# Attention exponentials behind the weights' copies, steps one product later, a new order in the last group, row factors on ScalarE

## The reference

```
proj = rms_norm(x, g_mix) @ w_in            # q,k,v,z,beta,a | qd,kd,vd | gate_a,gate_b
oa = gated_delta_rule(...)                  # chunked, with a triangular inverse per head
oa = rms_norm(oa, g_delta_out) * silu(za)
p  = softmax(qd @ kd^T / 8 + bias)          # two maps per head, 8 heads, causal
od = (p[0] - lam * p[1]) @ vd
od = rms_norm(od, g_subln) * (1 - lam_init) # per token and head
mix = sigmoid(gate_a + b0) * oa + sigmoid(gate_b + b1) * od
x = x + mix @ w_o
x = x + moe_ffn(rms_norm(x, g_ffn))         # top 4 of 32 experts, width 1024, clamped SwiGLU
```

## Time and profile before

| | |
|---|---|
| median of 3 runs | 1276.15 us (1274.95 to 1277.62) |
| the profiled execution | 1277.58 us, its span 1275.9 us, mean granted clock 0.997 |
| busy: PE, DVE, ACT, POOL | 1220.6, 391.1, 308.3, 43.3 us |
| moved | 465.59 MB, 364 GB/s over the span |
| chain that ended last | PE 65%, DMA 19%, DVE 5%, ACT 3% |
| largest lines of the chain | 2037 20%, loads of w_up 19%, 2084 14%, 1747 6%, 1978 and 1698 4% each |

### The profile page before, as it was taken

One profiled execution on the slowest core, in us unless ns is written; L12 is line 12 of the kernel. 1 busy time (PEld: TensorE's weight loads), 2 busy tenths in 40 slices (PEclk: granted clock), 3 DMA queues, 4 the chain that ended last, 5 costly groups with the idle time before them and its releaser, 6 DMA issues.

```text
span 1275.9 us, 14962 instructions
## 1 busy us (share of the span) xinstructions
PE 1220.6 (96%) x5558; PEld 535.2 (42%) x5558; DVE 391.1 (31%) x1041; ACT 308.3 (24%) x644; POOL 43.3 (3%) x100
## 2 busy tenths in 40 slices
PE   9999999999999999999999999999999999999997
PEld 7777456644443333333333333333333333333332
DVE  5776647479341221111221111221111112211111
ACT  3332222464222121121121112121121211111121
POOL 4401000000000000000000000000000000000000
PEclk9999999999999999999999999999999999999999
DMA  7644974698969999999999999999999999999997
GB/s 257 185 156 131 226 234 150 156 299 303 380 257 423 426 429 428 429 428 428 428 429 427 429 429 429 428 428 427 429 429 428 428 427 429 428 429 428 429 426 303
DMA packets 67582, 465.59 MB, mean 365 GB/s; under 512 B 11016, under 2 KB 14216, under 8 KB 42848
## 3 DMA queue, kind: packets, MB, share of 16 engines
q1 hardware_dynamic: 61768, 452.68, 86.1%
q0 software_dynamic: 5344, 11.95, 4.9%
q10 hardware_dynamic: 440, 0.58, 0.1%
HBM read 462.84 MB, written 1.97 MB: 364 GB/s over the span
## 4 chain that ended last, share of the span: by engine, by line
PE 65%; DMA 19%; DVE 5%; ACT 3%; issue 2%; SPq 1%; DVEq 0%; ACTq 0%
PE pb L2037 20%; DMA space<-in_w_up_dram 19%; PE pb L2084 14%; PE pb L1747 6%; PE pb L1978 4%; PE pb L1698 4%; PE pb L1678 3%; PE pb L1965 3%; PE pb L1892 2%; PE pb L1653 2%; PE pb L1972 1%; PE pb L1997 1%; DVE buf_a L1592 1%; DVE buf_a L1589 1%; DVE buf_a L1586 1%
## 5 line engine op out<-in xcount | busy, mean ns | idle before, releaser
L2037 PE MATMUL pb<-space,buf_a 128*64 128x512 f32 x2048 | 460.4, 595 | 16.1 <-DMA space<-in_w_up_dram 16.1
L2037 PEld LDWEIGHTS pb<-space,buf_a 128*64 128x64 f32 x2048 | 146.1, 137 | 285.3 <-issue 257.2
L1586 DVE TENSOR_SCALAR buf_a<-pb 128x256 f32<-128x256 f32 x64 | 26.9, 421 | 687.2 <-PE pb L2037 687.2
L2084 PE MATMUL pb<-space 128*64 128x512 f32 x1024 | 227.1, 595 | 7.3 <-ACT space L1114 7.3
L2084 PEld LDWEIGHTS pb<-space 128*64 128x64 f32 x1024 | 70.7, 137 | 140.9 <-issue 125.3
L1090 ACT ACT_TABLE_LOAD x32 | 41.1, 1283 | 222.4 <-PE pb L1965 222.4
L1678 PE MATMUL pb<-space 128*128 128x256 f32 x384 | 88.6, 384 | 1.0 <-ACT space L924 0.6
L1107 ACT ACTIVATE buf_a<-buf_a 128x256 f32<-128x256 f32 x64 | 26.7, 417 | 217.3 <-DVE buf_a L1586 217.3
L1678 PEld LDWEIGHTS pb<-space 128*128 128x128 f32 x384 | 71.3, 190 | 13.2 <-issue 2.4
L1116 ACT COPY space<-pb 128x512 f32<-128x512 f32 x32 | 18.7, 585 | 209.9 <-PE pb L2084 209.9
L1978 PE MATMUL pb<-space 64*128 64x512 f32 x264 | 65.6, 615 | 0.8 <-ACT space L1116 0.8
(11 more groups left out here) (322 smaller groups left out, 949.7 us busy)
## 6 DMA issues: line engine op xcount, KB each, us to landing
space<-in_w_up_dram SPq DMA_DIRECT2D x127, 2048.0 KB, 24.9
space<-in_w_down_dram SPq DMA_DIRECT2D x61, 2048.0 KB, 23.3
space<-in_w_in_dram SPq DMA_DIRECT2D x25, 1024.0 KB, 7.3
space<-in_w_in_dram SPq DMA_DIRECT2D x7, 2048.0 KB, 11.1
space<-in_w_in_dram POOLq DMA_DIRECT2D x8, 1024.0 KB, 10.7
space<-in_w_o_dram SPq DMA_DIRECT2D x4, 1024.0 KB, 5.2
space<-in_w_down_dram SPq DMA_DIRECT2D x4, 1024.0 KB, 29.2
xt<-in_x_dram SPq DMA_DIRECT2D x4, 512.0 KB, 8.9
```

Source lines behind the costliest of these rows:

```text
L1586: v.tensor_scalar(glu[:, cols], pairs[:, :, 0], LIMIT, None, ALU.min).then_inc(s_glu, 1)
L2037: ins = mm(up_out(hf, n_), xg[:, c, :], up_columns(line, hf, n_), start=False, stop=(c == KC - 1), skip_group_check=True)
L2084: ins = mm(pb[64 * hf:64 * hf + 64, 2, :], actT[:, c // 4 * 2 + c % 2, hf_in, :], slot(m)[:, at_:at_ + 512], start=(c == 0), stop=(c == KC ...
```

## The change

The delta rule's steps from `n2` on and all attention steps stand one product later (`nk` stays at 16, `ktd` goes from 17 and 18 to 18 and 19). The exponentials are a step of their own, `ex`, one step behind their logits and sorted behind the copy of the turned weights. The last group GB runs as P5, P1, P2, P6, P3, P7, P4, with P4 in the bank of P2 and opening its own sum, so that the mix's quarters come in the order `LAST_OUTS`, and `mt` for the second half of block 0 stands behind P7, that for the first half behind P4. In `odn`, ACT multiplies each head's output by its row factor, 12 and 4 activations, and DVE multiplies by the subln vector in two wide products. SP waits for P7 before it loads x again. The diff, cut:

```diff
@@ -67,15 +67,17 @@
     UNITS = ("P5", "P1", "P7", "P6", "P3", "P2", "P4")
+    LAST_UNITS = ("P5", "P1", "P2", "P6", "P3", "P7", "P4")
     HALVES = tuple((b, n, hf) for n in range(2) for b in range(NB) for hf in range(2))
     SEVEN = (KD, VD, GA, GB)
-    SEQ = [(g, name) for g in range(6) for name in (UNITS if g in SEVEN else HALVES)]
+    SEQ = [(g, name) for g in range(6) for name in (LAST_UNITS if g == GB else UNITS if g in SEVEN else HALVES)]
     AT = {u: i for i, u in enumerate(SEQ)}
     BANKS = {KD: {"P5": 0, "P3": 0, "P1": 7, "P6": 7, "P7": 6, "P4": 6, "P2": 1},
              VD: {"P5": 0, "P3": 0, "P1": 1, "P6": 1, "P7": 6, "P4": 6, "P2": 7},
              GA: {"P5": 0, "P3": 0, "P1": 2, "P6": 2, "P7": 3, "P4": 3, "P2": 1},
-             GB: {"P5": 0, "P3": 0, "P1": 1, "P6": 1, "P7": 3, "P4": 3, "P2": 2}}
+             GB: {"P5": 0, "P3": 0, "P1": 1, "P6": 1, "P7": 3, "P4": 2, "P2": 2}}
     PLACES = {KD: {"T": (6, 0), "T3": (6, 1), "B11": (8, 0), "B22": (8, 1), "B21": (9, 0)},
...
+    LAST_OUTS = (2, 1, 0, 3)
...
@@ -131,41 +134,43 @@
         put(3 + i, ("sb", 4 * i, min(4 * i + 4, 31)))
     put(9, ("qt", 0))
     put(10, ("qt", 1), ("nq",))
-    put(12, ("n2", 0))
-    put(13, ("n2", 1))
-    put(14, ("y1", 0))
-    put(15, ("y2", 0))
-    put(16, ("y3", 0), ("nk",))
-    put(17, ("yt", 0), ("ktd", 0))
...
-    put(29, ("osum",))
...
-    put(32, ("osc", 1))
-    put(34, ("oag",))
+    put(13, ("n2", 0))
+    put(14, ("n2", 1))
+    put(15, ("y1", 0))
+    put(16, ("y2", 0), ("nk",))
+    put(17, ("y3", 0))
+    put(18, ("yt", 0), ("ktd", 0))
...
+    put(30, ("osum",))
...
+    put(33, ("osc", 1))
+    put(35, ("oag",))
     for h in range(H):
-        put(19 + 2 * h, ("a1", h))
-        put(21 + 2 * h, ("aw", h))
-        put(22 + 2 * h, ("a2", h))
-        put(23 + 2 * h, ("a3", h))
-    put(35, ("odn", 0, 6))
-    put(38, ("odn", 6, 8))
-    put(39, ("oan",))
+        put(20 + 2 * h, ("a1", h))
+        put(21 + 2 * h, ("ex", h))
+        put(22 + 2 * h, ("aw", h))
+        put(23 + 2 * h, ("a2", h))
+        put(24 + 2 * h, ("a3", h))
+    put(36, ("odn", 0, 6))
+    put(39, ("odn", 6, 8))
+    put(40, ("oan",))
     for g in SEVEN:
         put(AT[(g, "P5")], ("grow", g, "B22"))
         put(AT[(g, "P6")], ("grow", g, "B21"))
     for i in after:
-        after[i].sort(key=lambda it: {"aw": 0, "a2": 0, "grow": 1, "a1": 3}.get(it[0], 2))
-    put(43, ("mt", 0), ("mt", 1))
+        after[i].sort(key=lambda it: {"aw": 0, "a2": 0, "grow": 1, "a1": 3, "ex": 3}.get(it[0], 2))
+    put(42, ("mt", 1))
+    put(43, ("mt", 0))
     sched = []
     extra = {3: [("ba",)], 4: [("bt",)], 6: [("gc",)], 8: [("gr",)], 10: [("E",)], 12: [("nc", 0)], 13: [("nt", 0)], 14: [("nr", 0)],
...
             load(4)
+            after_product(GB, "P7")
             for b in range(NB):
                 sp.dma_start(xt[:, b, :], x[0, b * P:(b + 1) * P, :]).then_inc(s_x[b], 16)
...
             COPIED = {"P5": 0, "P1": 2, "P6": 3}
             USED = {"P3": 0, "P2": 1, "P4": 2}
-            LAST_USED = {"P6": 0, "P3": 1, "P2": 2, "P4": 3}
-
-            def use(g, k):
+            LAST_USED = {"P2": (2, 1), "P3": (1, 3), "P7": (0, 4), "P4": (3, 5)}
+
+            def use(g, k, steps):
                 b, n_ = OUTS[k]
                 cols = slice(512 * n_, 512 * n_ + 512)
                 if g == VD:
                     return
-                act_e.wait_ge(s_cf, results(g, k + 2))
+                act_e.wait_ge(s_cf, results(g, steps))
                 if g == KD and k == 0:
                     act_e.wait_ge(s_red, 1)
                 if g == KD:
...
                     root(f"od{it[1]}", rsd[:, :, it[1]:it[2]], ow[:, :, it[1]:it[2]])
+                    act_e.wait_ge(s_gd, 4 if it[1] == 0 else 6)
+                    for b in range(NB):
+                        for h in range(it[1], it[2]):
+                            ins = sc.activation(OD_h[:, b, h], OD_h[:, b, h], ACT.Copy, scale=rsd[:, b, h:h + 1])
+                    ins.then_inc(s_gd, 1)
                 elif it[0] == "a2":
                     take_turned_weights(it[1])
...
+                        use(SEVEN[turn_of(g) - 2], 3, 5)
+                elif it[0] == "ex":
                     h = it[1]
                     act_e.wait_ge(s_nm, h + 1)
                     l = lgt[h % 2]
...
                 dve.wait_ge(s_pj, done[(g, name)])
-                if name == "P7":
+                if g == GB:
+                    if name == "P2":
+                        dve.wait_ge(s_pjf, taken[(g, "P1")])
+                        ins = v.tensor_tensor(c11, src, c11, ALU.add)
+                    elif name == "P6":
+                        dve.wait_ge(s_gm, 8)
+                        v.tensor_tensor(c12, gate_bias(g, 1), src, ALU.subtract)
+                        v.tensor_tensor(c22, c22, src, ALU.subtract)
+                        ins = v.tensor_tensor(c21, gate_bias(g, 3), src, ALU.add)
+                    elif name == "P3":
+                        dve.wait_ge(s_cf, results(g, 2))
+                        ins = v.tensor_tensor(c12, src, c12, ALU.add)
+                    elif name == "P7":
+                        v.tensor_tensor(c21, c21, src, ALU.add)
+                        ins = v.tensor_tensor(c22, c22, src, ALU.subtract)
+                    else:
+                        dve.wait_ge(s_cf, results(g, 4))
+                        ins = v.tensor_tensor(c21, src, c21, ALU.add)
+                    ins.then_inc(s_cf, 1)
+                elif name == "P7":
                     dve.wait_ge(s_pjf, taken[(g, "P5")])
...
                     link(v.tensor_scalar(part, part, 1.0 / P, EPS, ALU.mult, ALU.add))
                     roots(f"od{lo}", rsd[:, :, lo:hi], part, ow[:, :, lo:hi])
+                    dve.sem_inc(s_gd, 1)
                     if lo == 0:
                         dve.wait_ge(s_bup, 1)
+                    dve.wait_ge(s_gd, 5 if lo == 0 else 7)
                     for b in range(NB):
-                        for h in range(lo, hi):
-                            ins = v.scalar_tensor_tensor(out=OD_h[:, b, h], in0=OD_h[:, b, h], scalar=rsd[:, b, h:h + 1], in1=gsubr, op0=ALU.mult, op1=ALU.mult)
+                        ins = v.tensor_tensor(OD_h[:, b, lo:hi], OD_h[:, b, lo:hi], gsubr[:, None, :].to_broadcast([P, hi - lo, P]), ALU.mult)
                     link(ins)
                 elif it[0] == "oag":
...
                             dve.wait_ge(s_ml, 64)
                         take_with_bias(g, name, 0 if name == "P5" else 2)
                     elif name not in ("P5", "P1"):
+                        if g == GB and name == "P7":
+                            gate_product(GB, 1)
                         results_step(g, name)
                     if g == GA and name in ("P2", "P4"):
                         gate_product(GA, ("P2", "P4").index(name))
                     elif g == GB and name in ("P5", "P1"):
                         gate_product(GA, 2 + ("P5", "P1").index(name))
-                    elif g == GB and name in ("P3", "P2", "P4"):
-                        gate_product(GB, ("P3", "P2", "P4").index(name))
+                    elif g == GB and name in ("P3", "P4"):
+                        gate_product(GB, 2 if name == "P3" else 0)
                     if g == GB and name == "P4":
                         gate_product(GB, 3)
                 elif it[0] == "a1":
...
             def mix_turn(b, n_):
-                pe.wait_ge(s_mix, OUTS.index((b, n_)) + 1)
+                pe.wait_ge(s_mix, LAST_OUTS.index(OUTS.index((b, n_))) + 1)
                 if b:
-                    pe.wait_ge(s_mixT, n_ + 1)
+                    pe.wait_ge(s_mixT, 2 - n_)
                 else:
                     pe.wait_ge(s_ode, H)
...
                         pe.wait_ge(s_cf, results(g, 1))
                         pe.wait_ge(s_tadd, 2 * turn_of(g))
                     cols = quarter_at(g, q)
-                    opens = name in ("P5", "P1", "P7", "P2")
+                    opens = name in ("P5", "P1", "P7", "P2") or g == GB and name == "P4"
                     for c in range(4):
                         ins = mm(pb[:, bank, :], rows[:, c, :], cols[:, c, :], start=(opens and c == 0), stop=(c == 3), skip_group_check=True)
```

38 lines of the change are left out of this document (17 added, 21 removed).

## The result

The changed kernel takes 1281.33 us (median of 5 runs, 1278.03 to 1284.30) where the kernel before takes 1276.15 (1274.95 to 1277.62): a ratio of 1.0034, interval 1.0018 to 1.0050, so it is slower by 4.3 us by the ratio of paired runs, by 5.2 by the medians.

A forecast was written before the change was run, and what follows sets the result against it. TensorE was taken to bound the kernel up to the output projection, then expert-weight loads, the end following one to one. Gains 3.2 + 5.1 + 2.8 against 3.9 + 1.7 + 4.1 + 1.7 paid gave 1276.5 us, range 1271.8 to 1280.6.

The forecast's parts named there:

- Part 1: Steps one product later: stalls at the first head products and keys' scaling go, 5.4 less 2.2, gain 3.2 us.
- New stall 2.2: At VD's third product, TensorE waits 2.2 us for the third sum that POOL's adding transfer lands.
- nearest is no fall: Behind the 2.2 us stall at VD's third product the clock was taken to stay up, at no cost.
- Rival (c): VD's third sum lands 1.3 or more later, stall 3.5 with a clock fall: 2.8 more, 1279.3 us; chance 0.25.
- Part 2: Exponentials behind the copies of turned weights: all three stalls before attention outputs go, gain 5.1 us.
- Part 3: Row factors on ScalarE: TensorE waits 3.9 us before head 7's output, and the slow clock costs 1.7 more.
- T: The moment VectorE ends head 7's weights, from which the forecast counts ScalarE's and VectorE's work; 299.86 us before the change.
- Part 4: Last group's order: 4.1 us stall at the mix's first turn, 1.7 by the clock; tail gains 2.8.
- Rival (d): A switch of ScalarE's tables costs as much again before as the load: 2.6 more, 1279.1 us; chance 0.03.
- (a): The two TensorE stops form but the clock stays up: 3.4 less, 1273.1 us; chance 0.20.
- (b): VectorE is ahead, so neither TensorE stop forms: 11.4 less, 1265.1 us; chance 0.06.
- Rival (e): The end doesn't follow the output projection's start; the experts' loads hide all of it: 1276.2 us; chance 0.05.

The follow-up runs named there:

- the old order: Kernel before with later steps, exponentials behind the copies and VD's third sum begun ahead of the inverse's block loads, last group unchanged: 1267.64 us, ratio 0.9934.
- Parts 1 and 2 alone: Kernel before with only the steps one product later and the exponentials behind the copies: 1272.18 us, ratio 0.9964.
- the earlier sum: Changed kernel with VD's third sum begun ahead of the loads of the inverse's blocks: 1275.84 us, ratio 0.9997 to the kernel before.
- the repeat: Changed kernel measured once more with no edit: 1282.05 us, ratio 1.0043 to the kernel before.
- the kernel with parts 1 to 3: Kernel before with later steps, exponentials behind the copies and row factors on ScalarE, last group's old order kept: 1279.13 us, ratio 1.0010.
- filling: Changed kernel with idle matmuls, 12 before head 7's output and 14 before the mix's second-half turn: 1275.30 us, ratio 1.0002 to the kernel before.

## Why the prediction was right or wrong

The text said 1276.5 with no change as the likeliest (0.47) and gave slower 0.29. It came out slower: the median of 1281.33 is 0.7 above the upper end of 1280.6, the paired ratio, 1.0034 of 1276.15, gives 1280.5, just inside.

**Part 1 failed, in the term "New stall 2.2", "nearest is no fall".** The place was right: VD's third product, by POOL's transfer. The size was not. In the eight profiles that have SP's order of the change, the stall and the product's time behind it (3.60 at full clock) are 2.46 and 3.67, 2.73 and 3.67, 2.79 and 5.18, 2.96 and 5.14, 3.24 and 6.58, 3.44 and 6.61, 3.73 and 6.29, 3.85 and 6.15. With the slow clock that is 2.5 to 6.5 a run and 5.0 on average: 3.15 of idle time for the 2.2, and 1.8 by the clock for nothing. The run that took it away gained 5.9, in the old order 3.8. The other side of the part was a little larger than forecast: the slow clock behind the old stall had slowed the product behind it too, 1.72 in all and not 1.47, so 5.65 were gained and not 5.4. Instead of 3.2, part 1 gained 5.65 less 3.8 to 5.9: nothing to 1.9, and 0.7 by the average. Rival (c), the third sum late with a fall of the clock, was what happened. Its price of 2.8 more is what the eight profiles give on average (5.0 for 2.2), and by 1279.3 it named the nearest time of all. Its reason was borne out in direction: in all eight traces the transfer took 12.9 to 13.2 for 12.2, so 0.7 to 1.0 longer and not 1.3. That SP's quarters beside it are the cause is not shown. What makes the stall differ from run to run is mostly when the transfer is issued, 17.4 to 18.5 behind the product that starts at 156 us (18.1 before), as the quarter that it adds to lands sooner or later: the stalls of 2.46 and 2.73 belong to 17.4 and 17.5, those of 3.73 and 3.85 to 18.5 and 18.4. The mistake in method was to read the rows of 2.53 (fell) and 2.43 (did not) as an edge and to take the nearer side; there is no such edge.

**Part 2 was right** for TensorE: 0 stalls between 200 and 290 us, 5.06 gone. Parts 1 and 2 alone gave 4.6 (2.6 to 6.6), where their terms give 5.65 + 5.06 - 5.0 = 5.7 with the eight profiles' average, 4.8 with the earlier sum's 5.9 and 6.9 with the old order's 3.8. So the average fits, but the times don't tell these three apart by much.

**Part 3 was right.** Stop 3.9 forecast, 3.44 found; slow clock 1.7, found 1.69 (2.7 in the repeat). From T on (298.76): scalings' end T+5.2 for T+5.4, the copy's end T+7.5 for T+7.8, VectorE's wide products at T+7.1 for T+7.4. The sum of 5.6 was measured twice, 5.6 (4.5 by the other ratio) and 5.9; but the slow clock in it is as little fixed as in part 1: the same stop had none in the run with both turns behind the last product.

**Part 4 was right in the changed kernel.** At the mix's turn 4.07 for 4.1 and 1.69 for 1.7; the turn at T+28.0, which is T+26.4 with the slow clock of the first stop in it, as the text's remark has it. The forecast's own additions are slightly off: its terms add up to T+22.4 for TensorE and T+26.1 for VectorE, so to a stop of 3.7; that 4.1 lies so near the 4.07 found has some luck in it. Behind the last product 2.18 for 2.25, and the output projection at full clock. From the kernel with parts 1 to 3 (1.0010) to the changed one (1.0034 and 1.0043) it costs 3.1 to 4.2; the terms say 3.0. That the stop of 3.9 covers GB's quarter B21 was right too: without the stop it is 0.89 and 1.03 late.

**The table switches**: the load takes 1.28 and the tanh starts at 305.28, 0.02 after the load's end at 305.26, as in the earlier trace rows. Rival (d) has no support. Rivals (a) and (b) fell with the clock at 0.50 and the two stops; with the clock kept up by filling, the time was 5.2 shorter, where (a) priced it at 3.4. Rival (e) fell with the constant 936 to 938 between the output projection and the end.

With part 1 at nothing instead of 3.2 (the earlier sum's 5.9 as its cost), the sum is 3.5 slower, 0.27%; by the traces' average of 5.0 it is 2.8. Measured were 4.3 and 5.5, with intervals that begin at 2.3 and 3.8. So the mis-sized term accounts for most of the miss, and 0.8 to 2.7 us stay open; up to 1.0 of that is the slow clock behind head 7's stop, 2.7 in one trace for 1.7.

## What to carry to other kernels

When steps are moved later to hide one load, list every transfer that was hidden only because that load's stall came first, and move its issue in the same edit: here the first two parts with the earlier issue were worth 8.4 us, and without it 4.6. Work sent from a late engine to another is only a gain if nothing that a third engine waits for stands behind it there: VectorE was relieved of 3.24, idled 3.81 for it, and TensorE stood 3.44. And a stall of some 2 to 3 us before full-speed matmuls should be priced as a spread, once with and once without the slow clock; here even a stop of 3.44 cost anything from nothing to 2.7 us more.
